# Output gates and squares moved to ScalarE and GpSimd, layer 0's first norm by thirds, and cached values of four sequences per TensorE pass, in a two-layer hybrid decoder step

## What is computed

```python
h = rmsnorm(x); z = h @ w_in          # 8 attention heads and 8 mLSTM heads of 64
# group A: dilated window attention; prompt: banded, sample: over a cache of 2048 positions
# group B: mLSTM matrix memory, chunks of 128 tokens
h = num / jnp.maximum(jnp.abs(den), jnp.exp(-m_t))[..., None]
C_new = cw[..., None, None] * C + jnp.einsum('bhs,bhsv,bhsk->bhvk', ws, v, k)
og = jax.nn.sigmoid(ob)
ya = rmsnorm(o_a.reshape(B, T, W_A), g_a)
yb = og * rmsnorm(h_b, g_b)
x = x + jnp.concatenate([ya, yb], axis=-1) @ w_o
x = x + conv_glu(x)                   # up, causal conv of width 3, gelu gate, down
x = x + sigmoid(rmsnorm(x) @ w_gate) * (p @ w_proj)
```

## Time and profile before

| | |
|---|---|
| three executions | 3443.04, 3444.86, 3445.46 us; median 3444.86 us |
| the profiled execution | 3444.41 us; its span 3442.6 us |
| TensorE busy (PE) | 3191.4 us, 93% of the span |
| VectorE (DVE) / ScalarE (ACT) / GpSimd (POOL) busy | 2096.1 / 897.2 / 593.4 us |
| moved by DMA | 209.78 MB |

### The profile page before, as it was taken

The page is one execution under the profiler, slowest core; times in us unless marked ns, Lnnn a source line. Parts: engine busy times, 40 slices in busy tenths (PEclk is TensorE's granted clock), DMA queues, the critical chain, the costliest instruction groups (busy, mean ns, idle before and its releaser), DMA issues. The chain is left out here.

```text
span 3442.6 us, 48958 instructions
## 1 busy us (share of the span) xinstructions
PE 3191.4 (93%) x19573; PEld 2893.6 (84%) x19573; DVE 2096.1 (61%) x4518; ACT 897.2 (26%) x1789; POOL 593.4 (17%) x498
## 2 busy tenths in 40 slices
PE   6899899679999999999998998995899999999989
PEld 6777677469999999999987776772889999999988
DVE  5666476777555555557556654777675555555573
ACT  4333333213111111113233333321231111111131
POOL 1001111202122122211110110111022112212210
PEclk8999999789999999999999999997899999999999
DMA  5121123531111111110221111225211111111101
GB/s 155 35 55 51 44 70 71 170 99 50 37 50 50 50 38 50 49 49 19 88 58 45 49 44 42 72 80 173 71 62 50 50 38 50 50 50 38 48 24 66
DMA packets 208330, 209.78 MB, mean 61 GB/s; under 512 B 34628, under 2 KB 180996, under 8 KB 206000
## 3 DMA queue, kind: packets, MB, share of 16 engines
q1 hardware_dynamic: 208104, 206.66, 20.1%
HBM read 175.00 MB, written 31.61 MB: 60 GB/s over the span
## 5 line engine op out<-in xcount | busy, mean ns | idle before, releaser
L780 POOL TENSOR_TENSOR wlo<-raw,whi 128x512 fp32r<-128x512 f32 (+3 forms) x488 | 592.6, 1251 | 2792.5 <-ACT whi L1282 2792.5
L796 PE MATMUL ps<-hi,wlo 128*128 128x344 f32 x2880 | 933.1, 324 | 25.0 <-DVE wb L2137 15.5
L797 PE MATMUL ps<-lo,whi 128*128 128x344 f32 x2880 | 926.3, 322 | 0.0
L798 PE MATMUL ps<-hi,whi 128*128 128x344 f32 x2880 | 926.1, 322 | 0.0
L796 PEld LDWEIGHTS ps<-hi,wlo 128*128 128x128 f32 x2880 | 547.3, 190 | 28.2 <-DVE wb L2137 16.1
L797 PEld LDWEIGHTS ps<-lo,whi 128*128 128x128 f32 x2880 | 547.0, 190 | 0.6
L798 PEld LDWEIGHTS ps<-hi,whi 128*128 128x128 f32 x2880 | 546.8, 190 | 0.0
L796 PE MATMUL ps<-whi,lo 128*128 128x512 f32 (+5 forms) x1152 | 452.0, 392 | 21.6 <-ACT zt L1335 20.8
L798 PE MATMUL ps<-whi,hi 128*128 128x512 f32 (+5 forms) x1152 | 429.0, 372 | 0.0
L797 PE MATMUL ps<-wlo,hi 128*128 128x512 f32 (+5 forms) x1152 | 427.4, 371 | 0.0
L2149 DVE TENSOR_TENSOR X<-X,ps 128x344 f32<-128x344 f32 x528 | 268.7, 512 | 195.8 <-PE ps L798 195.3
(11 more groups left out here) (284 smaller groups left out, 3974.2 us busy)
## 6 DMA issues: line engine op xcount, KB each, us to landing
raw<-in_w_up SPq DMA_DIRECT2D x44, 1024.0 KB, 5.1
raw<-in_w_in SPq DMA_DIRECT2D x112, 256.0 KB, 4.5
raw<-in_w_down SPq DMA_DIRECT2D x22, 1024.0 KB, 4.9
kvb<-in_cache_win_k SPq DMA_DIRECT2D x48, 256.0 KB, 3.2
cache<-in_cache_win_v SPq DMA_DIRECT2D x42, 256.0 KB, 5.4
x_scratch<-X SPq DMA_DIRECT2D x8, 1032.0 KB, 6.6
X<-x_scratch SPq DMA_DIRECT2D x4, 2064.0 KB, 15.7
raw<-in_w_out SPq DMA_DIRECT2D x8, 1024.0 KB, 6.4
```

The source lines that it names most:

```text
L780: pool.tensor_tensor(out=wlo[:, s, r], in0=raw[:, s, r], in1=whi[:, s, r].bitcast(F32), op=ALU.subtract).then_inc(w_split, 1)
L796: nc.tensor.matmul(out, a_lo, b_hi, start=first, stop=False)
L797: nc.tensor.matmul(out, a_hi, b_lo, start=False, stop=False)
L798: return nc.tensor.matmul(out, a_hi, b_hi, start=False, stop=last)
```

## The change

1. **Start.** In layer 0 the squares and their sums follow each third of the split instead of standing after all three. The convolution vectors are loaded after x's tiles 3 to 5 and both first weight blocks, live in the raw slots 2 and 3 instead of `lo`, and are turned after tile 7. So blocks 2 and 3 are loaded after the four stores of X.
2. **Gates.** Exp, Ln(1 + .), Exp on ScalarE (`output_gates`) give the sigmoid; VectorE's 36 pairs of add and reciprocal a layer go. The product with the gate goes to GpSimd, 8 instructions a pair (`gated`), between the splits.
3. **Squares of the mLSTM output.** ScalarE squares each chunk with a running sum (`output_squares`); VectorE's four instructions at the end of a pair go. The attention half's row scales are made at the start of the last pair.
4. **Order at a pair's start.** The masked decay comes first on VectorE, by halves of 512 columns, then `prepare(0)`, then the scaled queries and the cleared state.
5. **Gains.** The output norms' gains are multiplied into the 4 `w_out` blocks on ScalarE (`scale_block`, 32 instructions of 128 x 256 a layer) instead of into y.
6. **y's tiles.** The row buffer `rowr` is a third place, so tiles 0 to 2 are loaded early; ScalarE scales the attention half of a tile (`y_first`), VectorE the other half in two pieces.
7. **Cached values.** Each product has 32 instead of 64 weight columns and goes to the 32 partitions of its sequence's group; four sequences stand side by side, 12 products in chunk 3 and 12 in chunk 5, in two banks. The own token's value makes a trip through `s_scratch` into that layout, in SyncE's order ahead of pieces 19 to 23.
8. `sample_max`, `sample_weights`, `sample_turned` move one chunk later; the stores of n, m and the memory's output move behind the loads of y.

```diff
             for t in range(3):
                 sp.dma_start(stages[t][0:rows(t), :], token_rows(t)).then_inc(staged[t], 16)
+            load_block(0)
+            load_block(1)
+            for t in range(3, 6):
+                sp.dma_start(stages[t][0:rows(t), :], token_rows(t)).then_inc(staged[t], 16)
             for l in range(DEPTH):
                 sp.dma_start(cs_rows(l, 0, 2 * NB), A["state_conv"][l]...
...
+                for t in range(3):
+                    load_y(t)
+                sp.dma_start(X[:, 0:4, :], Xd[:, 0:4, :]).then_inc(x_back[0], 16)
+                sp.wait_ge(*at(o_exp, PAIRS))
                 sp.dma_start(Zd[6, :, WA - P:WA], zt[0:NB, last % 2, NT, OG:ZW]).then_inc(z_stored[last % 2], 16)
                 sp.wait_ge(*at(z_stored[1], stored_value(last)))
                 sp.dma_start(mz[:, 2 * HD + 32:3 * HD], Zd[6].rearrange("b (r d) -> (b r) d", d=32)).then_inc(mo_in, 16)
+                sp.wait_ge(*at(own_done, 1))
+                sp.dma_start(Sd[2].rearrange("b (h d) -> (b h) d", d=HD), sv[:, 0, :]).then_inc(own_stored, 16)
+                sp.wait_ge(*at(own_stored, 16))
+                sp.wait_ge(*at(pz_set, 2))
+                for g in range(4):
+                    sp.dma_start(so[32 * g:32 * g + NH, :, :], Sd[2][g:NB:4, :].rearrange("j (h d) -> h j d", h=NH)).then_inc(so_in, 16)
+                sp.wait_ge(*at(v_used, 12))
                 for i in range(19, 24):
-                    sp.wait_ge(*at(v_used, i - 18))
                     load_values(i)
                 sp.wait_ge(*at(mem_done, 1))
...
+                def gated(q, first, last):
+                    pool.wait_ge(*at(o_exp, q + 1))
+                    for c in range(first, last):
+                        pool.wait_ge(*at(ysq_done, NT * q + c + 1))
+                        pool.tensor_tensor(out=yb[:, c, :], in0=yb[:, c, :], in1=zt[:, (PAIRS + q) % 2, c, OG:ZW],
+                                           op=ALU.mult).then_inc(yb_done, 1)
...
-                        for i in range(4 * c - 8, 4 * c - 4) if c >= 2 else ():
+                        if c not in (3, 5):
+                            return
+                        half = (c - 3) // 2
+                        for x in (0, 1):
+                            pe.wait_ge(*at(v_in[2 * half + x], 96))
+                        for r in range(3):
+                            for g in range(4):
+                                b = 4 * half + g
+                                a = (r * NB + b) * 32
+                                nc.tensor.matmul(ps[32 * g:32 * g + 32, 6 + half, :], pZ[:, a:a + 32], value_place(3 * b + r),
+                                                 start=(r == 0), stop=(r == 2)).then_inc(v_used, 1)
...
+                def output_gates(p):
+                    act.wait_ge(*at(z_done, (NT + 1) * (p + 1)))
+                    own = [zt[:, p % 2, 0:NT, OG:ZW], zt[0:NB, p % 2, NT, OG:ZW]]
+                    for og in own:
+                        do(nc.scalar.activation(og, og, ACT.Exp, scale=-1.0), wait=(og is own[1]))
+                    for og in own:
+                        do(nc.scalar.activation(og, og, ACT.Ln, bias=one1[0:og.shape[0], :]), wait=(og is own[1]))
+                    for og in own:
+                        do(nc.scalar.activation(og, og, ACT.Exp, scale=-1.0), o_exp if og is own[1] else None, wait=False)
+                def output_squares(q, c):
+                    act.wait_ge(*at(n_read, NT * q + c + 1))
+                    do(nc.scalar.activation(oa[:, :], yb[:, c, :], ACT.Square, accum_out=ysq[:, q, c:c + 1]), ysq_done)
...
+                        if c == 3 and q + 1 < PAIRS:
+                            output_gates(p)
+                        if c:
+                            output_squares(q, c - 1)
...
-                    y_squares(p, kT[:, :], slice(0, NT))
-                    do(v.tensor_tensor(out=yb[:, :, :], in0=yb[:, :, :], in1=zt[:, p % 2, 0:NT, OG:ZW], op=ALU.mult), yb_done)
...
                     if t < NT:
                         dve.wait_ge(*at(yst_in[t % 4], 16 * (t // 4 + 1)))
-                        parts = [(0, y[:, 0:WA], 0), (1, y[:, WA:D - P], WA), (1, yb[:, t, :], D - P)]
+                        do(v.tensor_scalar(y[:, WA:D - P], y[:, WA:D - P], rs, None, ALU.mult), wait=False)
+                        do(v.tensor_scalar(y[:, D - P:D], yb[:, t, :], rs, None, ALU.mult), yn_done, wait=False)
```

More of the change, by code:

```diff
@@ L529, in _ @@
                 sp.dma_start(cs_rows(l, 2 * NB + CW, 1), A["conv_b"][l:l + 1, :]).then_inc(cs_in, 16)
-            load_block(0)
-            for t in range(3, 6):
-                sp.dma_start(stages[t][0:rows(t), :], token_rows(t)).then_inc(staged[t], 16)
-            load_block(1)
             for t in range(6, NT + 1):
@@ L1276, in _, with scale_block, round_block, square @@
             do = Steps(act, act_step)
-            def round_block(g):
+            def scale_block(g, first, last):
+                s = g % NSLOT
+                act.wait_ge(raw_in[s], raw_value(g))
+                act.wait_ge(gout_in, 32 * (g // NBLK + 1))
+                for k in range(first, last):
+                    w = raw[:, s, k * 256:(k + 1) * 256]
+                    do(nc.scalar.activation(w, w, ACT.Identity, scale=gout[:, k:k + 1]), wait=(k + 1 == last))
+            def round_block(g, scaled=False):
                 s, used = g % NSLOT, BLOCKS[g % NBLK][3]
                 act.wait_ge(raw_in[s], raw_value(g))
+                if BLOCKS[g % NBLK][0] == "out" and not scaled:
+                    scale_block(g, 0, KT)
                 do(nc.scalar.activation(whi[:, s, 0:used], raw[:, s, 0:used], ACT.Copy), w_hi, wait=False)
-            def square(at, i, n):
-                c, k = squares_order(i)[n]
+            def square(at, i, n, l=1):
+                c, k = squares_order(i, l)[n]
                 sem, value = at(sq_used, 24 * i + n - 1)
@@ L1305, in _ @@
                         high(0, 0, c, k)
-                    if c < 2:
-                        round_block(c)
+                    if c == 0:
+                        round_block(0)
+                    for k in range(KT):
+                        square(since(0), 0, KT * c + k, 0)
+                elif t == 3:
+                    round_block(1)
             act.wait_ge(const_set, 6)
-            for n in range(24):
-                square(since(0), 0, n)
             for l in range(DEPTH):
@@ L1628, in _ @@
                         low(since(0), 0, 0, t // 3, k)
+                    for k in range(KT):
+                        add_square(since(0), 0, KT * (t // 3) + k, 0)
             dve.wait_ge(x_evac_a, NT + 1)
             dve.wait_ge(const_set, 6)
-            for n in range(24):
-                add_square(since(0), 0, n)
             for l in range(DEPTH):
@@ L1976, in _ @@
                             prepare(c + 1)
-                        if c == 0 and not last:
-                            dve.wait_ge(*at(o_exp, q + 1))
-                            output_gate(NT)
                         if not last:
-                            output_gate(c)
                             if c + 1 == NT:
```

279 lines of the change are left out of this document (157 added, 122 removed).

## The result

The change took the kernel from 3443.95 us (median of four runs, 3440.21 to 3445.46) to **3408.04 us** (four runs, 3404.01 to 3408.42): a ratio of 0.9895, 95% interval 0.9878 to 0.9912. The forecast was 3410. The profiled run of the new kernel took 3408.42 us, its span 3406.6, 36.0 less than before's 3442.6. The new kernel itself was not run there again, so a difference of a few us between medians of different chips says little.

What follows compares the result with a forecast made beforehand. TensorE was taken as the limit almost everywhere, with time to gain at the start and before each layer's output projection. Terms of 10.5 + 3.2 + 21.0 = 34.7 us off 3444.4 gave 3410 us, range 3378 to 3428.

Steps and rivals of the forecast that it cites:

- Part 1: Program start: TensorE's 8.9 us wait before the column sums shrinks by 8.0 and the clock stays up; 10.5 us less.
- its 11.4 before the discount: Start: gain from shorter wait and full clock, cut to 10.5 because x's tiles 6 to 8 arrive behind convolution rows.
- The bound of 12.5: Start: upper limit in us set for the gain there; the lower was 3.
- Part 2: First mLSTM pair: TensorE's 2.2 us wait for the masked decay shrinks by 1.6 us per layer, 3.2 in all.
- Part 3: Start of the last pair: masked decay ends at 650.2 for 670.6 us, `finish(0)` comes 18.9 us earlier.
- Part 4: Last pair, chunk 5: TensorE waits some 15 us for the last pieces of cached values, all there at 693.4.
- Part 5: Last pair: twelve packed 32-column products take 5.5 us if they overlap, 18.5 in a row; chunk 3's are hidden.
- Part 6: Chunk 5 to the output projection: projection starts at 729.0 for 739.49 us, 10.5 earlier, 21.0 for both layers.
- the GpSimd rival: Last pair: GpSimd and VectorE hold each other up, 0.58 us in each of eight chunks, 9 us; 3419, chance 0.07.
- the hold by transfers: Last pair: transfers delay the cached values for chunk 5; the rival without it gave 3380 us, chance 0.15.
- late in the mLSTM pairs: First three mLSTM pairs: rival that ScalarE's gates and squares delay evacuations, up to 53 us; 3463, chance 0.05.

Runs made afterwards that it cites:

- The experiment: New kernel with the start's squares and their sums put back behind the last third's splits, in one piece of 24: 3415.45 us.
- the idle copies: New kernel plus 32 idle copies of a 128 by 128 tile on VectorE ahead of the last pair's masked decay: 3408.35 us.
- the best order: New kernel with X's first-half load behind the last five pieces of cached values, and those issued ahead of the small round trips: 3385.37 us.
- the 3381 run: New kernel with X's half behind the last five pieces, those ahead of the small round trips, and the last weight split's preparation in chunk 4: 3380.95 us.

## Why the prediction was right, and where it was not

**Part 1, the start (10.5).** 12.3 came by the first mLSTM pair. The milestones held: first projection 40.9 (about 40), last sum at 50.2 (about 50), column sums at 51.3 without a wait, 1.96 us long (about 2.3). Where the prediction stops counting, 13 products behind the column sums, the lead is 11.0 (66.64 less 55.63), near its 11.4 before the discount; 1.3 more come on the way to the first pair and are not located. The bound of 12.5 held. The experiment shows what the prediction did not say: with the later rows alone the first projection starts 5.2 us sooner than before, and the early squares put it 7.2 later again, but take away the wait and the slow sums. The term is the sum of two, 6 to 7 us for the squares and 5 to 6 for the rest.

**Part 2, the first pair (1.6 per layer).** 1.1 in the new trace, 1.4 when undone alone. In the last pair it is worth nothing.

**Not in the sum: pairs 2 and 3.** I wrote that work which leaves VectorE there is worth nothing. They gained 0.9 us each, 3.8 in four: TensorE's wait of 0.9 us for an evacuation of the next projection, once in each of them, is gone. No run isolates its cause; that ScalarE's gates no longer stand between the evacuations is only argued. It is this row of the kernel before that has no fellow:

```profile
526.32 0.50 PE L796 MATMUL ps<-whi,lo 128*128 128x512 f32 x1 [0.90 <-ACT zt L1335]
```

**Part 3.** On the time scale of the kernel before (15.25 us added, the lead at the end of pair 3) the masked decay ends at 650.0 (650.2 predicted), `finish(0)` comes at 655.1 (655.2). The steps were right to 0.2 us, and worth little, as the idle copies show.

**Part 4, the new wait.** TensorE reached chunk 5 at 679.9 (678.5), the pieces were there at 693.3 (693.4), the wait was 13.4 and 14.5 us in the two layers ("some 15"). The mechanism, a small store that lands only with the transfers ahead of it, is borne out; its store took 13.7 us from issue to landing, 14 before. That the pieces came within 0.1 us of the time stated is luck: the terms given for them add up to 694.4, not to 693.4 (683.2, 2.1, four times 0.45, four gaps of 0.48, 5.4). In the run the reload went 0.7 later (683.9), the four small loads took 0.4 less, and the pieces were there 6.0 us after the first was issued, not 7.3. My remark that the list was about as long now was enough for the forecast, but its make-up wasn't understood: the runs give 4 us per layer to X's half and 7 to the round trips with an idle queue.

**Part 5, packing (5.5 us).** 4.9 us in chunk 5, at a mean granted clock of 0.55, so nearly all at 1.2 GHz as assumed; 4.5 in chunk 3.

**Part 6 (10.5 per layer).** This term was too large: the output projection came 8.4 us nearer in layer 0 and 6.7 in layer 1. On the same scale, chunk 5's products ended at 698.3 (698.9) and `finish(5)` came at 699.6 (701.0), 1.4 early, but `finish(7)` at 716.2, not 713.9; from there to the first turn of y it took 5.8 us (6.1), to the projection 9.1 more (9.0). The step that failed is the 5.5 us from `finish(5)` to `finish(6)`, "all VectorE work that stays", taken over from the kernel before: they were 9.0 us (684.33 to 693.36), while `finish(6)` to `finish(7)` took 7.6 for 7.4. The four small instructions of the sample memory, which stand there, cost 3.6 us more, because GpSimd's split of the last block, once in chunks 1 and 2, now lies over them (688.35 to 693.27); with the split moved away they take 0.92 us again. That is the GpSimd rival, which I had priced at 0.58 us a chunk and taken as another case; it came together with the forecast. Layer 1 has the same 3.6 us. Its further 1.7 are not one step: measured from the end of pair 3, the output projection was 1.2 us sooner there than in layer 0 before the change, and is 0.5 later now, with a wait for the pieces of 14.5 us for 13.4.

The sum, 34.7, missed the 36.0 of the spans by only 1.3 us, and that is luck, because its errors cancel: 1.8 too little at the start, 3.8 in pairs 2 and 3 and 0.8 unlocated between the layers, against 1.0 too much for the first masked decays and 4.1 from the last pairs on (2.1 in layer 0; in layer 1 3.8, of which 1.8 came back behind its output projection).

**The other rivals.** Without the hold by transfers the time was put at 3380; the best order with the split moved gives 3381, without it 3385. So near a hit is luck too: the rival had the last pair 25.5 us shorter than before (10.5 and 15), and in the 3381 run it is 21.8 and 20.7 us shorter (the stretch, 253.18 and 253.03 us, less the 1.9 us of pairs 2 and 3); gains at other places made it up. ScalarE is not late in the mLSTM pairs: TensorE's two waits for `zt` in each layer's pairs 2 and 3 are gone, and those of the whole span fell from 20.8 to 18.5 us, though the longest grew from 1.0 to 1.8.

## What to carry to other kernels

Before work is moved off an engine, follow the queue of transfers that its consumer needs: here, of 19 us by which VectorE started earlier, 13 turned into a wait for loads until these were put in order. A small store with a wait behind it is worth its place in the queue: issue everything big that is already free to go before waiting for it. When weights are split or rounded at another time, look at what small instructions lie beside it then.

## What was not expected of the hardware

- Loads at 344 GB/s with the 16 DMA engines 95% busy for 25 us; a 4 KB store issued behind them landed after 13.7 us, and after 9 with 2.1 MB less ahead. The Trainium skill ("DMA: Bandwidth & Descriptors", Queues, rings and completion order) says that a transfer's completion is written only after all earlier writes of the same DMA engine; the two landings agree.
- GpSimd's split also holds small VectorE instructions of one tensor operand. In the kernel with the late squares the first six instructions of the start's row scales (128 by 9, three of them with one tensor and immediate numbers) meet a split of eight steps, 54.79 to 62.53, and take 0.89 to 0.94 us each; the seven behind the split take 0.17, as all thirteen do in the new kernel, ahead of that split:

```profile
56.84 0.89 DVE L1692 TENSOR_SCALAR rcol<-yrs 128x9 f32<-128x9 f32 x1
```

- Of the Trainium skill ("SBUF — State Buffer", Who interferes with whom) I had weighed only the rule for two inputs in SBUF. The same section names `tensor_scalar` as able to use both ports and so to contend; two of the four slowed instructions of the last pair and this one are of that kind, and the rows agree.
- Both sides pay: a product of 2048 columns took 0.8 us more beside a split, the split 2.0 us more.
